# The 31-tap convolution of a Trainium2 kernel: shifts of 32 channels four at a time on TensorE

## The reference, cut to what matters

```python
CONV_WIDTH = 31

def dwconv(x, w, b):
    k, c = w.shape
    y = lax.conv_general_dilated(
        x, w[:, None, :].astype(x.dtype), window_strides=(1,),
        padding=[(k // 2, k // 2)], dimension_numbers=('NWC', 'WIO', 'NWC'),
        feature_group_count=c)
    return y + b

def conv_module(h, w_in, b_in, dw_w, dw_b, ln_g, ln_b, w_out):
    a, gt = jnp.split(h @ w_in + b_in, 2, axis=-1)
    u = a * jax.nn.sigmoid(gt)
    u = dwconv(u, dw_w, dw_b)
    u = layernorm(u, ln_g, ln_b)
    return jax.nn.silu(u) @ w_out
```

## Time and profile before

| | before |
|---|---|
| median of three runs | 3197.2 us |
| profiled execution | 3197.04 us |
| its span | 3195.2 us |
| PE busy in the span | 3138.7 us (98%) |
| DVE, ACT, POOL busy | 1441.0, 1255.7, 1541.2 us |
| granted clock of TensorE, mean | 0.997 of full speed |
| first convolution layer's input product | 656.4 to 800.0 us |
| second convolution layer's | 2636.2 to 2779.5 us |

### The profile page before, as it was taken

How to read it: one execution, slowest core, us unless ns; L and a number is a source line. 1 busy time by engine, 2 the same in 40 slices (tenths; PEclk the granted TensorE clock), 3 DMA queues, 4 the chain that set the end, 5 groups by cost and what they waited for, 6 DMA issues and landing times. The chain is left out here.

```text
span 3195.2 us, 34928 instructions
## 1 busy us (share of the span) xinstructions
PE 3138.7 (98%) x13891; PEld 2468.7 (77%) x13891; DVE 1441.0 (45%) x2678; ACT 1255.7 (39%) x1856; POOL 1541.2 (48%) x764
## 2 busy tenths in 40 slices
PE   8999999999999999999999999999999999999999
PEld 5668888866788887778888877787888886688887
DVE  5564111289633345446243523322534358953433
ACT  5463222255443335554343322222433335543332
POOL 3225545577354553334554533443455547555544
PEclk9999999999999999999999999999999999999999
DMA  5212332221232233222323322222232332133232
GB/s 183 76 47 86 100 99 95 97 73 53 76 103 92 93 105 103 90 86 91 101 93 99 111 68 72 73 86 66 93 101 91 99 99 66 40 95 104 93 99 86
DMA packets 80674, 286.03 MB, mean 90 GB/s; under 512 B 9088, under 2 KB 9344, under 8 KB 80384
## 3 DMA queue, kind: packets, MB, share of 16 engines
q1 hardware_dynamic: 80512, 283.80, 27.5%
HBM read 281.40 MB, written 2.10 MB: 89 GB/s over the span
## 5 line engine op out<-in xcount | busy, mean ns | idle before, releaser
L2362 POOL TENSOR_TENSOR WL<-RAW,WH 128x1024 fp32r<-128x1024 f32 x504 | 1216.2, 2415 | 1289.5 <-ACT WH L1642 1289.3
L1388 PE MATMUL PS<-XH,WH 128*128 128x512 f32 x2640 | 1069.7, 405 | 29.3 <-DVE PD L1926 15.5
L1390 PE MATMUL PS<-XH,WL 128*128 128x512 f32 x2640 | 1031.1, 391 | 0.0
L1389 PE MATMUL PS<-XL,WH 128*128 128x512 f32 x2640 | 1030.8, 390 | 0.0
L1642 ACT ACTIVATE WH<-RAW 128x1024 fp32r<-128x1024 f32 x504 | 529.3, 1051 | 544.8 <-PE PS L1390 455.7
L1388 PEld LDWEIGHTS PS<-XH,WH 128*128 128x128 f32 x2640 | 497.5, 188 | 169.4 <-issue 44.0
L1389 PEld LDWEIGHTS PS<-XL,WH 128*128 128x128 f32 x2640 | 497.8, 189 | 113.6 <-issue 15.8
L1390 PEld LDWEIGHTS PS<-XH,WL 128*128 128x128 f32 x2640 | 497.2, 188 | 105.2
L1388 PE MATMUL PS<-HH,WH 128*128 128x512 f32 x1264 | 494.8, 391 | 7.0 <-DVE HL L2260 4.4
L1389 PE MATMUL PS<-HL,WH 128*128 128x512 f32 x1264 | 493.2, 390 | 0.0
L1390 PE MATMUL PS<-HH,WL 128*128 128x512 f32 x1264 | 493.0, 390 | 0.0
(11 more groups left out here) (244 smaller groups left out, 2394.6 us busy)
## 6 DMA issues: line engine op xcount, KB each, us to landing
RAW<-wst SPq DMA_DIRECT2D x504, 512.0 KB, 3.5
BI<-natb SPq DMA_DIRECT2D x16, 384.0 KB, 4.4
X<-xin SPq DMA_DIRECT2D x16, 256.0 KB, 5.1
X<-cmpw SPq DMA_DIRECT2D x1, 2048.0 KB, 9.7
out<-X SPq DMA_DIRECT2D x8, 256.0 KB, 2.0
BI<-relm SPq DMA_DIRECT2D x4, 448.0 KB, 10.1
PRM<-prm SPq DMA_DIRECT2D x1, 685.0 KB, 12.5
BI<-rope SPq DMA_DIRECT2D x2, 256.0 KB, 4.0
```

The costliest lines, as they stand in the source:

```text
L1388: e.matmul(o, wh, h, start=first, stop=False)
L1389: e.matmul(o, wh, l, start=False, stop=False)
L1390: t = e.matmul(o, wl, h, start=False, stop=last)
L2362: e.tensor_tensor(WL[:, b % NSPLIT, :], RAW[:, b % NRAW, :], WH[:, b % NSPLIT, :].bitcast(f32), SUB).then_inc(*did(lo_made, ("lo", b)))
```

## The change

TensorE's share is now counted in fours: chunk c has `FOURS[c]` of them, each four taps. A buffer `four` in the room of `PT` holds, for each set x of 32 channels, four copies of these channels' gated row block, shifted by 0, 1, 2 and 3 columns and stacked on the four quarters of the partitions. One product with a 128x32 matrix (four stacked 32x32 diagonals) then adds four taps for 32 channels; four products, x = 0 to 3, write to the four quarters of the bank's partitions and so use the four column quarters of TensorE's array. The copies are laid out by 16 transfers of 32 rows for each chunk, from `PD` to `PT`, issued by SP. There is one buffer `four`, free again when TensorE's taps of the chunk are done. All shares move: TensorE 40 to 84 taps for each layer (40 products to 84, of 128x32 weights), POOL 63 to 46, DVE 145 to 118. TensorE's taps come 10 macs behind the odd group instead of 5, and in the last chunk three warming products stand ahead of them. ACT's diagonals become 84 of 128x32 for each layer instead of 40 of 128x128.

```diff
-TAPS_PE = (2, 3, 3, 4, 3, 4, 5, 16)
-TAPS_POOL = (8, 8, 8, 8, 8, 8, 8, 7)
+FOURS = (2, 2, 2, 2, 2, 2, 4, 5)
+TAPS_POOL = (6, 6, 6, 6, 6, 6, 6, 4)
...
-                diag = Ring([PT[:, i, j, :] for i in range(2) for j in range(4)], (*pt_free[0], *pt_free[1]))
+                room = PT[:, :, :, :].rearrange("p a b n -> p (a b n)")
+                four = Slot(None, room[:, 0:2128].rearrange("p (g n) -> p g n", n=532), (*pt_free[0], *pt_free[1]))
+                diag = Ring([room[:, 2128 + 256 * j:2384 + 256 * j] for j in range(7)], (*pt_free[0], *pt_free[1]))
...
+                    fours = ("fours", ci, c)
+                    width = 508 + n_pe
+                    for x in range(4):
+                        for y in range(4):
+                            fetch(four.ap[32 * y:32 * y + 32, x, 0:width], pad.ap[32 * x:32 * x + 32, y:y + width],
+                                  fours_in, fours, ch["u"], *four.free)
+                    four.free = (ch["pe"],)
+
                     def pe_taps():
-                        step("pe_taps", dgs, dg_made, pad.ap, ch["u"], ch["acc"].ap, ch["acc"].free,
+                        if c == 7:
+                            keep_warm(3)
+                        step("pe_taps", dgs, dg_made, four.ap, fours, ch["acc"].ap, ch["acc"].free,
                              None if c < 2 else ("pivot", ci), ch["pe"])
...
-                    later(pe_taps, 5, first=True)
+                    later(pe_taps, 10, first=True)
...
-                for j in range(len(dgs)):
-                    t = e.matmul(bk, dgs[j], pad[:, j:j + T], start=j == 0, stop=pivot_made is None and j == len(dgs) - 1)
+                for j in range(0, len(dgs), 4):
+                    for x in range(4):
+                        t = e.matmul(bk[32 * x:32 * x + 32, :], dgs[j + x], four[:, x, j:j + T], start=j == 0,
+                                     stop=pivot_made is None and j == len(dgs) - 4)
...
-                    ins = e.activation(dg, ident, ACT.Copy, scale=t)
+                    ins = e.activation(dg, cc("stack", 32), ACT.Copy, scale=t)
```

More of the change, by code:

```diff
@@ L36 @@
 )
-CONSTS = (("ident", 128), ("ones", 128), ("bones", 128), ("mask", ML), ("rowmask", 1))
+CONSTS = (("ident", 128), ("ones", 128), ("bones", 128), ("mask", ML), ("rowmask", 1), ("stack", 32))
 def offsets(spec):
@@ L183, in build @@
         gw_in, w1_in, w2_in, swap_in = sem("gw_in"), sem("w1_in"), sem("w2_in"), sem("swap_in")
+        fours_in = sem("fours_in")
         bias_in = [sem(f"bias_in{i}") for i in range(4)]
@@ L951, in pool_taps @@
                 def pool_taps(ch, a, b):
-                    j0 = TAPS_PE[ch["c"]]
+                    j0 = 4 * FOURS[ch["c"]]
                     for n in range(a, b):
@@ L968, in dve_taps @@
                     c = ch["c"]
-                    j0 = TAPS_PE[c] + TAPS_POOL[c]
+                    j0 = 4 * FOURS[c] + TAPS_POOL[c]
                     step("dve_taps", ci, c, a, b, ch["own"].ap, ch["own"].free, ch["two"].ap, ch["two"].free, ch["pe"],
@@ L974, in finish @@
                     c = ch["c"]
-                    n = 31 - TAPS_PE[c] - TAPS_POOL[c]
+                    n = 31 - 4 * FOURS[c] - TAPS_POOL[c]
                     dve_taps(ch, n // 2, n)
@@ L1025, in diagonals @@
                 def diagonals(c):
-                    n = TAPS_PE[c]
-                    dg = [diag.get() for _ in range((n + 3) // 4)]
-                    dgs = [dg[j // 4].ap[:, 128 * (j % 4):128 * (j % 4) + 128] for j in range(n)]
+                    n = 4 * FOURS[c]
+                    dg = [diag.get() for _ in range((n + 7) // 8)]
+                    dgs = [dg[j // 8].ap[:, 32 * (j % 8):32 * (j % 8) + 32] for j in range(n)]
                     i = step("diagonals", dgs, [tap(c, j) for j in range(n)], [x for s in dg for x in s.free])
@@ L1033, in evac @@
                     c = m // 2
-                    n_pe = TAPS_PE[c]
+                    n_pe = 4 * FOURS[c]
                     if m % 2 == 0:
@@ L1564, in pivot_sum, with pe_taps @@
                 e.matmul(d, HL[:, 7, 0:128], HH[:, 7, :], start=True, stop=True).then_inc(*did(pe_made, ("pivot_sum", ci)))
-            def pe_taps(i, dgs, dg_made, pad, u_made, bk, bk_free, pivot_made, event):
+            def pe_taps(i, dgs, dg_made, four, four_made, bk, bk_free, pivot_made, event):
                 for x in bk_free:
@@ L1569, in pe_taps @@
                 w.wait_ge(*at(dg_made))
-                w.wait_ge(*at(u_made))
-                for j in range(len(dgs)):
-                    t = e.matmul(bk, dgs[j], pad[:, j:j + T], start=j == 0, stop=pivot_made is None and j == len(dgs) - 1)
+                w.wait_ge(*at(four_made))
+                for j in range(0, len(dgs), 4):
+                    for x in range(4):
+                        t = e.matmul(bk[32 * x:32 * x + 32, :], dgs[j + x], four[:, x, j:j + T], start=j == 0,
+                                     stop=pivot_made is None and j == len(dgs) - 4)
                 if pivot_made is not None:
@@ L1834, in diagonals @@
             def diagonals(i, dgs, taps, free):
+                w.wait_ge(*at("cst2"))
                 for event in free:
@@ L2445, in constants @@
     c["rowmask"] = (q >= 31).astype(float)[:, None]
+    c["stack"] = np.tile(np.eye(32), (4, 1))
     cst = np.concatenate([c[n] for n, _ in CONSTS], axis=1).astype(np.float32)
@@ L2550 @@
     p["conv_b_in"] = cols(g["conv_b_in_2"])
-    p["conv_dw_w"] = g["conv_dw_w_2"].reshape(2, 31, 8, 128).transpose(3, 0, 2, 1).reshape(128, 496)
+    dw = []
+    for i in range(2):
+        for c in range(8):
+            w = g["conv_dw_w_2"][i, :, 128 * c:128 * c + 128]
+            n = 4 * FOURS[c]
+            dw.append(w[0:n].reshape(-1, 4, 4, 32).transpose(1, 3, 0, 2).reshape(128, n))
+            dw.append(w[n:].T)
+    p["conv_dw_w"] = np.concatenate(dw, axis=1)
     p["conv_dw_b"] = cols(g["conv_dw_b_2"])
```

## The result

The changed kernel takes 3332.6 us (median of 4 runs, 3331.28 to 3333.36), the kernel before 3197.5 beside it: a ratio of 1.0419, 95% interval 1.0401 to 1.0437. It is slower, as forecast, and by 135 us where 105 were forecast. The profiled execution's span is 3330.8 us.

What follows compares the result with a forecast made beforehand. PE, busy in 98% of the span, bounds the kernel, with DVE binding too in the first layer's input product. 3197.0 + 88 for both layers' longer beats + 16 for the slow clock = 3301, written 3302 us; range 3275 to 3335.

Steps and rivals of the forecast that it cites:

- The chain: Per chunk, scaling, sigmoid, rounding, weight load, 16 transfers, PE's taps, DVE's taps in sequence: a beat of 23.0 us.
- Scaling to the first transfer: DVE's scaling through sigmoid, rounding and rest of the block until SP is free, 4.9 us, plus the load's issue, 0.4.
- The relief of DVE, POOL and PE: Less work in both layers, such as 35.6 us of DVE, buys nothing because all three engines wait for SP.
- rival 3: Transfers land before PE comes to the taps; both layers save up to 17 us, 3180 us; chance 0.02.
- signs named ahead: Gatings 22 to 25 us apart, PE's longest waits on transfers, DVE waiting about 6 us before tap 1, transfers 0.57 apart.
- The issue spacing: SP's 16 transfers per chunk issue 0.57 us apart, taken from two copies within the chip's buffers; bounds 0.38 and 0.64.
- Rival 1: SP issues the small transfers faster, 0.38 or 0.47 us apart: 3256 or 3278 us; chance 0.13.
- The landing: The last of a chunk's 16 transfers lands in 2.3 us; first issue to last landing 10.8 us.
- The fours: Four column quarters of PE run side by side; chunks 0 to 5 cost 1.7 + 0.2 us, from a row of two halves.
- the rule of the Trainium skill: Weight loads overlap running products only where row groups differ, so 16 loads per chunk would be added; the prediction followed the row.
- The clock: PE's waits halve the clock for its taps, up to 1.7 us in each of 16 places; +16, bounds 0 and 27.
- The first beat and the tail: Each layer's first beat 20.0 us instead of 12.65, +7.4; behind the last gating PE's taps end after 17.8 us, +3.

Runs made afterwards that it cites:

- run 1: Changed kernel with TensorE's tap products reading the padded buffer, not waiting for the 16 transfers, which are still made (shifts wrong): 3183.4 us, ratio 0.9948 to the kernel before.
- Run 3: Changed kernel with SP's weight load of each chunk put behind the 16 transfers instead of ahead: 3288.3 us, ratio 1.0278 to the kernel before.
- run 4: Changed kernel with seven full warming products ahead of the fours in every chunk, in place of three in the last: 3316.7 us, ratio 1.0365 to the kernel before.
- Run 5: Changed kernel with all four products of a four writing the first column quarter, each overwriting it: 3443.7 us, ratio 1.077 to the kernel before.
- run 7: Changed kernel with one 128-row transfer per channel group, four a chunk for 16, same bytes, weight load behind them: 3210.4 us, ratio 1.0037 to the kernel before.
- last run of experiment 8: Two whole transfers on SP, two on ACT, with SP's two weight loads issued only once the copies landed: 3202.2 us, ratio 1.0009 to the kernel before.
- first run of experiment 8: Changed kernel with four whole transfers a chunk, two issued by SP and two by ACT, weight load behind them: 3245.7 us, ratio 1.0143 to the kernel before.

## Why the prediction came out as it did

**The chain.** Right, link by link. Scaling to the first transfer: 5.3 reckoned, 5.35 measured. The relief of DVE, POOL and PE bought nothing, as run 1 shows from the other side: with the wait gone the kernel is 14 us faster than before, near the 17 of rival 3. Run 3 shows the held load as part of the chain. Of the signs named ahead, PE's longest waits were on the transfers, once a chunk, as said. The gatings were 22 to 25 us apart by forecast and 25.2 to 27.0 measured, and DVE's waits before tap 1 in chunks 1 to 6 some 6 us by forecast and 9.3 to 13.2 measured. The terms below account for the longer beat; but the forecast's own sum, a beat of 23.0 us with 14.8 of DVE's work in it, left 8 us for that wait and not 6.

**The issue spacing.** Taken 0.57 us from the pair `TT<-TT`; measured 0.628 ((10.01 - 0.59) / 15). Its upper bound was 0.64. 15 x 0.058 x 16 chunks is 14 us too few. Rival 1, cheap issues, is out. The landing was 2.0 and not 2.3, 5 us too many in the sum, which by luck hid part of the rest.

**The fours.** Side by side, as the row of two halves had it: 1.92 us at the full clock (run 4) for 1.7 + 0.2. The weight loads lie within the passes there too. Run 5 shows the same with one quarter for all, so here too the measurement disagrees with the rule of the Trainium skill that the prediction weighed (TensorE: Matmul & The Clock Gate, Part 3, The mechanism). The same section of the Trainium skill also lets a load into a background weight buffer go ahead of running products; the records here do not tell whether that is what happened.

**The clock.** This term was mis-sized. I took three in five of 16 places at 1.7 us, 16 us, and 27 as the end of the range. In all 16 places the half level took most of the fours' time (the stretches around them have a mean of 0.50 to 0.59 in the first layer's first seven chunks, 0.70 in its last): the twelve chunks of two fours 3.24 to 3.64 us for 1.93, the seventh chunks 6.2 and 5.3 for 3.64, the last ones 6.3 and 7.4 for some 4.5. That is 29 us, 13 above my value and 2 above my bound, since I priced the long fours of the last two chunks like short ones. PE stood still for 5.5 to 9.1 us before them in the first seven chunks of a layer, where I had reckoned 6.5. Run 4 bears it out with 16 us, nearly all from nine places.

**The first beat and the tail.** 24.2 us for 20.0, and 20.2 for 17.8. In the first, POOL was still rounding when the gating was done, and the copies began 2.7 us behind it, not 1.1; the rest is spacing and clock.

**The sum.** 14 + 13 - 5 make 22 of the 30 us that were missing, and the held first transfers of both layers 3 more; some 5 us are left. Of these 1.8 stand in SP's timeline, where three rows of 16 transfers took longer than 10.1 us: this one, and two of 10.23:

```profile
742.52 11.33 SPq L2406 DMA_DIRECT2D PT<-PD  x16
```

The last 3 us no run took apart. The measured time lies at the upper end of the forecast's own range of 3275 to 3335, since spacing and clock both came out near their dear bounds.

**The rule on issuing.** The prediction weighed the Trainium skill (DMA: Bandwidth & Descriptors, Issuing engines are not separate DMA queues), by which starting a transfer is usually cheap beside the transfer. Per transfer that holds here (0.6 us against 2.0); in a row of 16 the issues are 9.4 of 11.5 us, and quartering their number (run 7) gave 78 us.

## What to carry to other kernels

Many small copies on one queue cost their issues in a row, about 0.6 us each here, and what is queued ahead of them: count issues in the chain from producer to consumer before bytes, and look at which waiting instruction stands before them. Fold shifts into one transfer's access pattern, and once issues are few, keep the big loads out of the same microseconds. An engine relieved of work gives nothing when all of them wait for the same landing.

## What the runs showed of the chip

- The rows of an issue: 0.60 us for 64 rows, 0.63 for 32, 1.05 for 128 rows written from 32 rows read four times. Such a read with overlapping windows works in a plain transfer.
- Bytes moved at nearly full use of the 16 DMA engines (last two columns of the rows below): copies within the chip's buffers alone 277 GB/s (last run of experiment 8), copies and weight loads together 272 (first run of experiment 8), weight loads from memory alone 369 (run 7). Two 0.5 MB loads issued 1.2 us behind the copies cost the kernel 44 us.

```profile
699.00:702.00 3.00, 3.00 (x15) 2.47 (x14) 3.00 (x5) 3.00 (x10) 2.86 (x3) 1.00 0.98 277
708.00:709.90 1.90, 1.89 (x17) 0.46 (x17) 1.52 (x3) 0.00 (x0) 1.76 (x3) 1.00 0.95 369
```

- The idle time before the fours does not settle their clock by itself. In run 4, behind seven products at the full clock, 2.3 us or less left the short fours at the full clock (1.92 us), and 2.7 to 4.5 us put most of them at half (2.9 to 3.64 us). In run 7, behind the input products, 2.02 us left them at the full clock, but 1.98 us put most of them at half:

```profile
708.01 1.92 PE L1597 MATMUL PS<-PT 128*32 128x512 f32 x16 [2.02 <-DMA PT<-PD]
...
2693.43 3.61 PE L1597 MATMUL PS<-PT 128*32 128x512 f32 x16 [1.98 <-DMA PT<-PD]
```
